# Whole fp32 conditioning weights, 8 KB expert rows, moved taps and a join by chunks of heads

## What is computed

```python
mod = silu(c) @ w_ada + b_ada                       # 6 x 1024 columns: shift, scale, gate, twice
u   = x * (1 + scale) + shift                       # also for the 256 context tokens
q, k, v, g, glu, gates = split(u @ w_in + b_in)     # 40 MB of weights
z   = depthwise_conv(za * sigmoid(zb), taps=31)     # along the tokens
h   = layernorm(ALPHA * x + gate_m * merge(retention(q, k, v), g, z, gates))
u2  = h * (1 + scale_f) + shift_f
for e in range(32):                                 # top 2 of 32 experts for each token
    y += combine[:, e] * (silu(u2 @ w_exp_gate[e]) * (u2 @ w_exp_up[e])) @ w_exp_down[e]
h   = layernorm(ALPHA * h + gate_f * y)
# second block: a gated MLP (24 + 8 MB), then attention with 16 heads over 3 dilated
# groups, each with its own softmax; the groups are merged by their maxima and sums:
m = min_g(negmax_g); e_g = exp(m - negmax_g); o = sum_g(e_g * acc_g) / sum_g(e_g * s_g)
out = layernorm(h + (o * z) @ b_w_out)              # residual and gains as in the kernel
```

## Time and profile before

| what | value |
|---|---|
| three timed runs | 1803.31, 1809.26, 1816.59 us; median 1809.26 |
| profiled execution | 1801.9 us |
| its span | 1800.1 us, 23483 instructions |
| mean granted clock of TensorE | 0.957 |
| bytes read from HBM | 379 MB |

### The profile page before, as it was taken

The page is one execution under the profiler, slowest core; times in us unless marked ns, Lnnn a source line. Parts: engine busy times, 40 slices in busy tenths (PEclk is TensorE's granted clock), DMA queues, the critical chain, the costliest instruction groups (busy, mean ns, idle before and its releaser), DMA issues.

```text
span 1800.1 us, 23483 instructions
## 1 busy us (share of the span) xinstructions
PE 1626.2 (90%) x8957; PEld 1327.1 (74%) x8957; DVE 1225.6 (68%) x1529; ACT 1005.3 (56%) x1099; POOL 466.7 (26%) x134
## 2 busy tenths in 40 slices
PE   4999999989995599999999999969898899999966
PEld 3788888877774477777777777748787688888754
DVE  5677666796566689999999999972721663636243
ACT  4523335435642578888888888854343345545631
POOL 0000000100000111111111111135776586656531
PEclk9999999999998699999999999989998899999978
DMA  7632234246766289999999999946544455353410
GB/s 276 195 117 94 82 132 140 95 142 211 257 226 222 94 315 346 355 343 358 350 347 360 353 350 357 359 179 206 198 146 139 149 188 166 115 164 118 141 59 24
DMA packets 194597, 380.99 MB, mean 212 GB/s; under 512 B 9302, under 2 KB 11134, under 8 KB 194526
## 3 DMA queue, kind: packets, MB, share of 16 engines
q1 hardware_dynamic: 194526, 380.02, 60.8%
HBM read 378.95 MB, written 1.05 MB: 211 GB/s over the span
## 4 chain that ended last, share of the span: by engine, by line
PE 64%; DMA 15%; DVE 11%; issue 5%; ACT 4%; POOL 0%; SPq 0%; DVEq 0%; POOLq 0%; ACTq 0%
DMA ring<-in_w_exp_down 13%; PE ps L719 11%; PE ps L720 10%; PE ps L726 10%; PE ps L1087 6%; PE ps L1092 5%; PE ps L887 2%; PE ps L886 2%; PE ps L893 2%; PE ps L783 2%; ACT w_hi L2341 1%; PE ps L1241 1%; DVE xs L1902 1%; DVE arena L1337 1%; DVE w_lo L1415 1%
## 5 line engine op out<-in xcount | busy, mean ns | idle before, releaser
L2341 ACT ACTIVATE w_hi<-ring 128x2048 fp32r<-128x2048 f32 x154 | 293.0, 1913 | 357.1 <-PE ps L726 209.6
L2640 ACT ACTIVATE w_hi<-ring 128x2048 fp32r<-128x2048 f32 x192 | 367.3, 1914 | 72.4 <-DMA ring<-in_w_exp_gate 48.3
L1897 DVE TENSOR_TENSOR w_lo<-ring,w_hi 128x2048 fp32r<-128x2048 f32 x192 | 397.2, 2104 | 13.4 <-ACT w_hi L2640 13.4
L2262 POOL TENSOR_TENSOR w_lo<-ring,w_hi 128x2048 fp32r<-128x2048 f32 x71 | 333.6, 4722 | 194.1 <-ACT w_hi L2341 193.8
L1415 DVE TENSOR_TENSOR w_lo<-ring,w_hi 128x2048 fp32r<-128x2048 f32 x83 | 189.6, 2287 | 110.9 <-ACT w_hi L2341 110.0
L2247 POOL TENSOR_TENSOR w_lo<-ring,w_hi 128x1024 fp32r<-128x1024 f32 x32 | 91.4, 2858 | 498.1 <-ACT w_hi L2640 498.1
L719 PE MATMUL ps<-w_hi,xt_hi 128*128 128x512 f32 x512 | 202.8, 396 | 4.9 <-ACT w_hi L2341 4.9
L720 PE MATMUL ps<-w_hi,xt_lo 128*128 128x512 f32 x480 | 188.0, 392 | 0.0
L1087 PE MATMUL ps<-w_hi,xs 128*128 128x512 f32 x512 | 147.5, 410 | 22.2 <-DVE xs L1902 21.9
L1092 PE MATMUL ps<-w_lo,xs 128*128 128x512 f32 x512 | 146.1, 408 | 3.4 <-DVE w_lo L1897 1.7
L719 PE MATMUL ps<-w_hi,yt_hi 128*128 128x512 f32 x352 | 140.4, 399 | 6.7 <-issue 3.1
(11 more groups left out here) (323 smaller groups left out, 2894.2 us busy)
## 6 DMA issues: line engine op xcount, KB each, us to landing
ring<-in_w_exp_gate SPq DMA_DIRECT2D x64, 1024.0 KB, 6.9
ring<-in_w_exp_up SPq DMA_DIRECT2D x64, 1024.0 KB, 10.3
ring<-in_w_exp_down SPq DMA_DIRECT2D x64, 1024.0 KB, 8.9
ring<-in_w_in SPq DMA_DIRECT2D x40, 1024.0 KB, 5.1
ring<-in_b_w_in SPq DMA_DIRECT2D x40, 1024.0 KB, 5.1
ring<-in_w_ada SPq DMA_DIRECT2D x24, 1024.0 KB, 5.8
ring<-in_a_w_in SPq DMA_DIRECT2D x24, 1024.0 KB, 6.1
ring<-in_w_ret_out SPq DMA_DIRECT2D x8, 1024.0 KB, 5.2
```

Of the source, the lines that this page charges most:

```text
L1897: dve.tensor_tensor(w_lo[:, p, 0:upto], ring[:, p, 0:upto], w_hi[p][:, 0:upto, :].bitcast(F32), ALU.subtract).then_inc(S("lo_ready"), 1)
L2262: pool.tensor_tensor(w_lo2[:, slots_of[n]], ring[:, slots_of[n]], w[:, :, :].bitcast(F32), ALU.subtract).then_inc(S("w_lo_full"), 1)
L2341: act.activation(part_of(n)[1][:, :, :], ring[:, slots_of[n]], ACT.Copy).then_inc(S("w_hi_full"), 1)
L2640: act.activation(w_hi[p][:, :, :], ring[:, p], ACT.Copy).then_inc(S("hi_ready"), 1)
```

## The change

Five edits, in different stages:

1. `row_unit` takes a unit whole, in fp32, out of the ring: it waits for the DMA alone and makes 4 products with a stationary operand of 32 columns (`s_cols`, both vectors 16 times), each of the 4 rows of a unit into a quarter of the partitions; `c_pick` adds the quarters. ACT's `lead` and DVE's `lo_of` go for all 24 units `ada` and `tail`; `lead` now names single units.
2. Gate and up units are loaded with rows `(p k)`, one piece of 8 KB a partition; a down unit is 256 full rows, two a partition, also 8 KB. `down_product` makes both halves of the columns from each unit, so both outputs are complete after the second. The order of h's columns (`h_parts`, two instructions instead of one on ACT and on POOL) and of the gate and up results (`rows_by_pair`) follows.
3. Taps move from before the gate into the k, v and q units.
4. POOL's gains move from behind the experts to behind the second expert.
5. Block b: columns in the order q0, k0, q1, k1, v0, v1 for each group and z at the end; the groups' attention starts in slots 3, 9 and 14; the join runs by chunks of four heads on DVE, with one exp each on ACT, in slots 15 to 19; the output units come in the order (0,0), (1,0), (0,1), (1,1), with the turn in two halves.

```diff
-BCOLS = list(range(12)) + [12, 13, 14, 15, 18, 19, 16, 17]
-BKIND = (["q", "q", "k", "k", "v", "v"] * 2) + ["q", "q", "k", "k", "z", "z", "v", "v"]
+BCOLS = [6 * g + c for g in range(3) for c in (0, 2, 1, 3, 4, 5)] + [18, 19]
+BKIND = ["q", "k", "q", "k", "v", "v"] * 3 + ["z", "z"]
 BGROUP = [0] * 6 + [1] * 6 + [2] * 8
-BIDX = [0, 1] * 10
+BIDX = [0, 0, 1, 1, 0, 1] * 3 + [0, 1]
...
+    steps = {t: [] for t in range(20)}
+    for g, first in ((0, 3), (1, 9)):
         for c in range(4):
-
-            for stage, name in enumerate(("scores", "turn", "values")):
-                if first + c + stage < 19:
-                    after[first + c + stage].append(((2 - stage, c), name, g, c))
-
-    steps = {t: [s[1:] for s in sorted(a)] for t, a in after.items()}
-    steps[18] = [s for s in steps[18] if s[0] != "values"]
-    steps[19] = [("values", 2, 0), ("turn", 2, 2), ("scores", 2, 3), ("values", 2, 1), ("turn", 2, 3), ("values", 2, 2), ("values", 2, 3)]
+            for stage, name in ((2, "values"), (1, "turn"), (0, "scores")):
+                steps[first + c + stage].append((name, g, c))
+    for t in range(14):
+        steps[t].sort(key=lambda s: (("values", "turn", "scores").index(s[0]), s[2]))
+    steps[14] += [("scores", 2, 0)]
+    steps[15] += [("turn", 2, 0), ("scores", 2, 1)]
+    steps[16] += [("turn", 2, 1), ("scores", 2, 2)]
+    steps[17] += [("values", 2, 0), ("turn", 2, 2), ("values", 2, 1), ("scores", 2, 3)]
+    steps[18] += [("values", 2, 2), ("turn", 2, 3)]
+    steps[19] += [("values", 2, 3)]
...
+        first["b_out"] = len(units)
+        for j in range(2):
+            for t in range(2):
+                stream_unit("b_out", a["b_w_out_2"][0], t, t, j)
...
-                return a["w_exp_down"][0, bass.ds(e, 1), :, W * j:W * (j + 1)].rearrange("e (k p) c -> p (e k) c", p=P)
+                return a["w_exp_down"][0, bass.ds(e, 1), 2 * P * j:2 * P * (j + 1), :].rearrange("e (p k) c -> p (e k c)", k=2)
             w = a["w_exp_gate"] if kind == "gate" else a["w_exp_up"]
-            return w[0, bass.ds(e, 1), HALF_K * j:HALF_K * (j + 1), :].rearrange("e (k p) c -> p (e k) c", p=P)
+            return w[0, bass.ds(e, 1), HALF_K * j:HALF_K * (j + 1), :].rearrange("e (p k) c -> p (e k c)", k=UC)
...
-                m, w = part_of(n)
-                pe.wait_ge(S("w_hi_full"), m + 1)
+                k = slots_of[n]
+                pe.wait_ge(S("w_full%d" % k), 16 * fills[n])
                 for c in range(UC):
-                    pe.matmul(o[:, 0, :], s_[:, UC * j + c].rearrange("p a b -> p (a b)"), w[:, c, :], start=(j == 0 and c == 0), stop=False)
-                remainder_ready(pe, n)
-                for c in range(UC):
-                    mm = pe.matmul(o[:, 0, :], s_[:, UC * j + c].rearrange("p a b -> p (a b)"), w_lo2[:, slots_of[n], c, :],
-                                   start=False, stop=(j == 1 and c == UC - 1))
+                    quarter = slice(32 * c, 32 * (c + 1))
+                    mm = pe.matmul(o[quarter, 0, :], s_[:, UC * j + c].rearrange("p a b -> p (a b)"), ring[:, k, c, :], start=(j == 0), stop=(j == 1))
...
+            def down_product(j, n, rd, shared):
+
+                p = SLOT_OF["down"] + j
+                for part, sem in ((w_hi[p], "hi_ready"), (w_lo[:, p], "lo_ready")):
+                    pe.wait_ge(S(sem), n + PER_ROUND * rd)
+                    for r in range(2):
+                        if sem == "lo_ready" and j == 1 and r == 1:
+                            pe.wait_ge(S("pool_lo"), shared)
+                        for half in range(2):
+                            mm = pe.matmul(ps[:, 2 + half, :], hs[:, 2 * j + r, :], part[:, 2 * r + half, :],
+                                           start=(sem == "hi_ready" and j == 0 and r == 0), stop=(sem == "lo_ready" and j == 1 and r == 1))
+                mm.then_inc(S("unit_done" + suffix(rd)), 1)
...
+            def turn_output(c):
+                pe.wait_ge(S("b_o_ready"), c + 1)
                 turn(("oT", c), lambda tt, j: b_z[:, tt, W * c + P * j:W * c + P * (j + 1)], "oT_turned")
-            for c in range(2):
-                pair_evacuated(pe, ("oT", c))
-            for t in range(2):
-                gemm_parts("b_out", t, ("b_out", t), ot_hi, ot_lo, half="y_half" if t else None)
+
+            turn_output(0)
+            pair_evacuated(pe, ("oT", 0))
+            gemm_unit("b_out", 0, 0, ot_hi, ot_lo)
+            turn_output(1)
+            gemm_unit("b_out", 1, 0, ot_hi, ot_lo)
+            pair_evacuated(pe, ("oT", 1))
+            gemm_unit("b_out", 0, 1, ot_hi, ot_lo)
+            gemm_unit("b_out", 1, 1, ot_hi, ot_lo, half="y_half")
...
+            def conditioning(cols):
+                link(dve.tensor_copy(cols[:, :, 0, :], sT[:, 0:KC].unsqueeze(2).broadcast_to([P, KC, 16])))
+                dve.tensor_copy(cols[:, :, 1, :], sT[:, KC:2 * KC].unsqueeze(2).broadcast_to([P, KC, 16])).then_inc(S("s_ready"), 1)
...
-            conv_taps(12)
+            conv_taps(20)
...
-            conv_taps(16)
+            conv_taps(22)
             for t in range(1, 4):
                 lo_of("v", t, 0)
-                conv_taps(16)
+                conv_taps(19)
                 lo_of("v", t, 1)
-                conv_taps(16)
+                conv_taps(22 if t == 1 else 27)
...
-            conv_taps(14)
+            conv_taps(18)
             lo_of("q", 0, 1)
-            conv_taps(4)
+            conv_taps(11)
...
+            def join_ahead(c):
+                dve.wait_ge(S("b_maxed"), 4 * (8 + c) + 4)
+                dve.wait_ge(S("b_probs"), 4 * (8 + c) + 4)
+                settle()
+                q = heads_of(b_q, c)
+                one(dve.tensor_tensor(q, heads_of(b_nm[:, 0], c), heads_of(b_nm[:, 1], c), ALU.min))
+                one(dve.tensor_tensor(q, q, heads_of(b_nm[:, 2], c), ALU.min))
+                for g in range(DIL):
+                    ins = dve.tensor_tensor(heads_of(b_e[:, g], c), q, heads_of(b_nm[:, g], c), ALU.subtract)
+                    if g == 2:
+                        ins.then_inc(S("b_ediff"), 1)
+                    else:
+                        link(ins)
+                dve.wait_ge(S("b_eexp"), c + 1)
+                for g in range(DIL):
+                    link(dve.tensor_tensor(heads_of(b_s[:, g], c), heads_of(b_s[:, g], c), heads_of(b_e[:, g], c), ALU.mult))
+                settle()
+                one(dve.tensor_tensor(q, heads_of(b_s[:, 0], c), heads_of(b_s[:, 1], c), ALU.add))
+                one(dve.tensor_tensor(q, q, heads_of(b_s[:, 2], c), ALU.add))
+                one(dve.reciprocal(q, q))
+                for g in range(DIL):
+                    link(dve.tensor_tensor(heads_of(b_e[:, g], c), heads_of(b_e[:, g], c), q, ALU.mult))
+                settle()
+                for g in range(2):
+                    pair_evacuated(dve, ("values", g, c))
+                    v = heads_of(b_acc[:, g], c)
+                    link(dve.tensor_tensor(v, v, heads_of(b_e[:, g], c).unsqueeze(3).broadcast_to([P, NT, 4, HD]), ALU.mult))
+                settle()
+                one(dve.tensor_tensor(heads_of(b_acc[:, 0], c), heads_of(b_acc[:, 0], c), heads_of(b_acc[:, 1], c), ALU.add))
+
+            def join_last(c):
+                dve.wait_ge(S("b_valued"), 8 + c + 1)
+                v = heads_of(b_acc[:, 2], c)
+                freed(dve.tensor_tensor(v, buf(("values", 2, c))[:, :, 0:256].rearrange("p t (h d) -> p t h d", h=4),
+                                        heads_of(b_e[:, 2], c).unsqueeze(3).broadcast_to([P, NT, 4, HD]), ALU.mult), ("values", 2, c))
+                pair_evacuated(dve, ("values", 2, c))
+                one(dve.tensor_tensor(heads_of(b_acc[:, 0], c), heads_of(b_acc[:, 0], c), v, ALU.add))
+
+            def gate_output(i):
+                pair_evacuated(dve, ("b", 18 + i))
+                v = b_z[:, :, W * i:W * (i + 1)]
+                dve.tensor_tensor(v, v, b_acc[:, 0].rearrange("p t h d -> p t (h d)")[:, :, W * i:W * (i + 1)], ALU.mult).then_inc(S("b_o_ready"), 1)
...
+                for act, g, c in slots[t]:
+                    if act == "turn" and g == 2:
+                        join_ahead(c)
+                if BKIND[t] == "z":
+                    gate_output(BIDX[t])
...
+                for e in range(2):
+                    half(e, False)
+                if rd == 0:
+                    pool.wait_ge(S("load_gains"), 48)
+                    for dst, row in ((gain0, ln2_g), (bias0, ln2_b)):
+                        pool.tensor_tensor(dst, row, pre0, ALU.mult).then_inc(S("gains_ready"), 1)
+                with pool.Fori(2, NE - 1) as e:
...
-            pool.tensor_tensor(h_rest, h_tok, h_parts[0][:, :, :], ALU.subtract).then_inc(S("h_left"), 1)
+            for tt in range(NT):
+                ins = pool.tensor_tensor(h_rest[:, tt, :].rearrange("p (j k q) -> p j q k", j=2, k=UC), h_tok[:, tt, :].rearrange("p (j q k) -> p j q k", j=2, k=UC),
```

(31 more changed lines are left out.)

159 lines of the change are left out of this document (41 added, 118 removed).

## The result

The changed kernel takes 1752.14 us in the median of 4 runs (1749.86 to 1753.45); the kernel before takes 1806.28 in its four. The ratio is 0.9693, with a 95% interval from 0.9645 to 0.9741. The forecast was 1744 with a range of 1722 to 1778. The profiled execution took 1751.8 us, 50 less than that of before; the sum had 65.

A forecast was written before the change was run, and what follows sets the result against it. Expert stage: PE, DVE and DMA within a few per cent, gate-unit waits last; second block: PE; tail: a DVE chain. Terms sum to -65.4: 1801.9 profiled becomes 1736.5, plus 7.4 for the median gives 1744, range 1722 to 1778.

The forecast's parts named there:

- Conditioning at the start: Eight conditioning units before glu: without copy and remainder they come as they land, glu's first product near 44: -11 us.
- Row products in the output stage: 16 conditioning units there: products 2.1 us a unit for 1.9, offset by fewer waits, 0 net; -2.5 at the stage's end.
- all four at once: Lower bound for a unit's four row products: all quarters overlap, 0.85 us a unit, -16 us in the output stage.
- Rival A: Row products in the quarters run one after another: +25 us in the output stage, +7.6 at the start, 1776; chance 0.14.
- Taps: Convolution taps moved from before the gate into DVE's gaps in the k, v and q units: -9.9 us.
- Expert rows: Expert weights in 8 KB pieces: period from 17.81 to 17.3 us, -16 in all; h's reordered parts +1.
- Rival B: The expert stage gains nothing because PE or DVE is last already: +16 us, 1760; chance 0.13.
- Rival C: Pieces of 8 KB move slower than 2 KB and bind the expert stage; at 300 GB/s 1862 us; chance 0.03.
- Gains: POOL's gains moved from behind the last expert to behind the second: 4.2 us gained, 2 given back, -2.2.
- Join: Second block's join by chunks and new unit order, covering PE's wait before the output turn: -24.8 us.
- Rival D: The join stalls PE in the slots of group 3 of the second block: +20 us, 1764; chance 0.14.
- I add 2: Cost of the chunk join's DVE and ACT work beside POOL's remainders in slots 15 to 18: 2 us, making -26.8 into -24.8.

The follow-up runs named there:

- run 1: Changed kernel with the row-product edit undone (24 conditioning units split again, products of 128 columns): 1774.48 us, ratio 0.9838 to the kernel before.
- run 2: Changed kernel with a unit's four row products put into two quarters of the partitions instead of four: 1759.72 us, ratio 0.9765 to the kernel before.
- run 7: Changed kernel with the taps edit undone, 46 taps before the gate again: 1756.93 us, ratio 0.9753 to the kernel before.
- run 3: Changed kernel with the expert-weight edit undone (2 KB pieces, old down units and order of h): 1757.61 us, ratio 0.9759 to the kernel before.
- run 4: Changed kernel with the permuted copies walked to write neighbouring values and read strided ones: 1744.58 us, ratio 0.9685 to the kernel before.
- run 5: Changed kernel with neighbouring writes in the permuted copies and expert units in 4 KB pieces: 1741.82 us, ratio 0.9688 to the kernel before.
- run 8: Changed kernel plus neighbouring writes and last slots' and output units' remainders on DVE, with POOL's gains behind the last expert again: 1728.57 us; gains in second expert, 1728.53.
- run 10: Changed kernel with the remainders for slots 16 to 19 and the output units on DVE instead of POOL: 1733.6 us, ratio 0.9618 to the kernel before.
- run 6: Changed kernel with expert transfers described row by row, meant as 2 KB pieces but sent as 8 KB: 1750.56 us, ratio 0.9719 to the kernel before.
- run 12: Changed kernel plus neighbouring writes, last slots' and output units' remainders on DVE, and 4 KB expert pieces: 1724.21 us, ratio 0.9566 to the kernel before.

## Why the prediction was right, and where its steps were not

The time lies in the range and 8 us above the forecast. Much of that closeness is luck. Two errors of opposite sign nearly cancel: the output stage gave 14.6 us more than forecast, the second block 17.3 less. The other steps were 12.5 us too hopeful together, so the profiled sums differ by 15.3 us. Half of these is hidden again by the 7.4 us that I added for the median of the runs before; they did not show in the changed kernel, whose profiled execution is at its median. With the output stage as forecast, the time would have been about 1767.

- **Conditioning at the start: right, a little large.** -8.5 for -11; run 1 has 7.8. The units came as they landed, with waits of 0.7 to 1.8 for DMA. Glu's leading copy starts at 41.40 for the 41.5 of the sum. What I left out is ACT's order: the evacuation of the last row product stands behind the leading copy of glu, which waited 5.28 us for its own DMA, so PE stood 5.00 before the columns. The two waits that I priced were real.
- **Row products in the output stage: the term was mis-sized.** "I take one pass's offset for each, 5 x 0.43 = 2.1", 0 net. A unit takes 1.06 us and two take 1.92, the bound that I had called "all four at once". 16 units by 0.87 are the 13.9 us of PE's busy time in run 1, and waits are the other 3.2 of its 17.1, where I had 4.3 and 2.5 at the end of the stage. Rival A is refuted by run 2, from the other side: it costs only where products share a quarter. The 1.4 us by the factor in the Trainium skill, an estimate, was nearer than my 2.1 and also too long.
- **Taps: right at their place.** 9.9 us in run 7, 7.02 of them the one wait. DVE's gaps held all 46 taps (none is left before the gate), and PE waits for no remainder there.
- **Expert rows: right in the period, wrong around it.** Period 17.31 for 17.3, with room in the DMA and PE at 98.7%. The price of the side effect was not: "POOL's first subtract [...] becomes two strided ones: +1, from 0 to +4" looked at POOL (4.05 to 5.68, a right guess) and took ACT's two for free. ACT's strided write costs 7.4 us. On the path to the first expert it and POOL's second instruction take 6.3 us by run 3, 4.7 of them by run 4. Rival B falls: the wait for gate units was the last one. Rival C has nothing for it: 8 KB do not move slower than 4 KB, by the estimate of run 5.
- **Gains: nothing.** The give-back of 2 was 3.2 in run 8, the gain of 4.2 was 1.75. The remainder behind the last expert takes 2.29 us again, as forecast, but DVE now waits 7.63 us for ACT's leading part ahead of it, and 4.78 before. The last expert also pays for the new layout (2.6 us, run 3), so that the stretch to the turn is as long as before.
- **Join: the cover failed.** Rival D came true. It was priced at +20; the term fell 17.3 us short, of which run 10 gets back 14.8 by the profile and 17 by the medians. "I add 2", with a bound of -5, rested on POOL being idle a third of the stage. The row I had, 4.23 us beside a remainder, said what one meeting costs; the step left out is when they meet. ACT makes the leading parts of the next slot right behind the exp that DVE waits for (1693.47 and 1693.60), and with them POOL's remainders start just as DVE begins the long products of the join (1695.58 and 1695.07). So the meetings are certain, not one in three: about 10.6 us of DVE in each of the four chunks, where 2.0 are needed. Run 10 moves POOL's remainders to DVE itself, and the time falls all the same.

What stays open: why pieces of 2 KB move 352 GB/s in the expert stage, at a busy share of 0.994, and 386 in the conditioning stage, at a share of 1.049. A share above 1 also says that the rates divided by it are rough. Whether the length of a piece decides or that its rows are neighbours in memory is not shown: run 6 was to separate the two, and its pieces stayed at 8 KB.

## What to carry to other kernels

In these runs an instruction of two SBUF operands on DVE and a POOL remainder do not share time (0.69 us becomes 4.88). When work is moved into a stage where POOL runs, ask which event starts POOL and whether the same event starts DVE. A permuted layout must be paid in somebody's copy: write neighbours and read with the stride, and put a row on every engine that issues such a copy, not on one of them. Products that fill only 32 columns are worth splitting by k over the four quarters (1.06 us for four of them).

## What the runs showed of the hardware that was not expected

- Four fp32 products of 32 columns in four quarters take as long as one: 1.06 us for eight passes, 1.02 for two. With two quarters, in the order 0, 0, 1, 1, it is 1.92, and with the next unit in the other two quarters 1.94 for both.
- An ACT copy of 128 x 1024 float32 to bf16 takes 0.95 us with neighbouring values (half of 1.90 for 128 x 2048, run 3), 1.06 when it reads every second (run 12), 1.96 when it reads every fourth (run 4), and 4.65 when it writes every 128th (the changed kernel). For results of 128 x 512 in float32 the strided write took 1.12 us instead of 0.59.
- Two DVE instructions that need 1.3 us together took 5.7 beside POOL's remainders, the next of 0.69 took 4.9; each ended within about 1 us behind one of POOL's pieces of 4.8. An instruction with one operand in PSUM is not held. DVE's timeline of the kernel before, while POOL makes two remainders from 1653.99 to 1663.11:

```profile
1656.84 0.75 DVE L2147 SCALAR_TENSOR_TENSOR arena<-ps,arena 128x512 f32<-128x512 f32 x1 [6.11 <-PE ps L726]
1657.51 0.87 DVE L2151 SCALAR_TENSOR_TENSOR arena<-ps,arena 128x256 f32<-128x256 f32 x2
1658.29 0.74 DVE L2147 SCALAR_TENSOR_TENSOR arena<-ps,arena 128x512 f32<-128x512 f32 x1
```

The instruction behind them, with both operands in SBUF, is that of the earlier trace rows.
